# A two-block network kernel on one core: an attention loop and a recurrence are reordered on five engines

## What is computed

```python
def rwkv7_recurrence(r, decay, k, v, a, b):
    """S_t = S_{t-1} diag(decay_t) + (S_{t-1} a_t) b_t^T + v_t k_t^T ;  y_t = S_t r_t."""
...
y = rwkv7_recurrence(rh, dh, kh, vh, -kk, kk * ah)
y = ((y - mu) * lax.rsqrt(var + LNX_EPS)).reshape(B, S, D)
y = y * lnx_w.astype(f32) + lnx_b.astype(f32)
bonus = jnp.sum(rh * kh * r_k.astype(f32), axis=-1, keepdims=True) * vh
y = y + bonus.reshape(B, S, D)
out = (y * g.astype(f32)).astype(w_o.dtype) @ w_o
...
# forgetting attention, 16 heads, two query blocks of 128
s = einsum(q, k) * scale + cum_log_f[q] - cum_log_f[k]
o = softmax(where(causal, s, -inf)) @ v
```

## Time and profile before

| | |
|---|---|
| median of 3 runs | 3367.44 us (3367.32 to 3367.82) |
| the profiled execution, its own time | 3353.73 us |
| its span, first to last instruction | 3352.1 us |
| PE busy | 3220.3 us, 96% |
| DVE busy | 2284.5 us, 68% |
| ACT busy | 1507.4 us, 45% |
| POOL busy | 353.0 us, 11% |
| mean granted TensorE clock | 0.962 of 2.4 GHz |

### The profile page before, as it was taken

One profiled execution on the slowest core, in us unless ns is written; L12 is line 12 of the kernel. 1 busy time (PEld: TensorE's weight loads), 2 busy tenths in 40 slices (PEclk: granted clock), 3 DMA queues, 4 the chain that ended last, 5 costly groups with the idle time before them and its releaser, 6 DMA issues.

```text
span 3352.1 us, 65137 instructions
## 1 busy us (share of the span) xinstructions
PE 3220.3 (96%) x23206; PEld 2785.1 (83%) x23206; DVE 2284.5 (68%) x3387; ACT 1507.4 (45%) x2115; POOL 353.0 (11%) x526
## 2 busy tenths in 40 slices
PE   7999999989998999999999999999999999999998
PEld 6887777878877888888888888888778888888887
DVE  6657666578776776776666767776566766666675
ACT  5543443456645554444443434444344434444343
POOL 2001022000124432100000000200011000000002
PEclk9999999989998888999999999999899999999999
DMA  6654545446761110466666666677435666666664
GB/s 191 171 148 114 138 138 170 132 138 175 210 190 47 34 34 25 139 179 187 185 191 185 191 185 188 176 188 188 119 114 150 181 192 184 191 184 189 186 183 144
DMA packets 1001281, 524.25 MB, mean 156 GB/s; under 512 B 25750, under 2 KB 996396, under 8 KB 1000620
## 3 DMA queue, kind: packets, MB, share of 16 engines
q1 hardware_dynamic: 995756, 507.99, 53.9%
q0 software_dynamic: 4560, 13.05, 1.1%
q10 hardware_dynamic: 816, 1.11, 0.1%
HBM read 513.69 MB, written 8.39 MB: 156 GB/s over the span
## 4 chain that ended last, share of the span: by engine, by line
PE 83%; DVE 8%; issue 4%; ACT 3%; POOL 1%; DMA 0%; ACTq 0%; DVEq 0%; POOLq 0%; SPq 0%; PEldq 0%
PE proj L302 47%; PE proj L304 24%; ACT w_high L271 1%; DVE w_low L258 1%; DVE g L312 1%; DVE w_low L274 1%; PE side L2232 1%; PE side L808 1%; POOL g L1954 0%; PE side L2281 0%; DVE g L2478 0%; DVE g L2702 0%; DVE g L2698 0%; PE side L2362 0%; PE side L2369 0%
## 5 line engine op out<-in xcount | busy, mean ns | idle before, releaser
L302 PE MATMUL proj<-b_pair,w_high 128*128 128x512 f32 x3872 | 1382.7, 401 | 22.8 <-DVE b_pair L1078 8.9
L302 PE MATMUL proj<-a_pair,w_high 128*128 128x512 f32 x3664 | 1293.4, 397 | 39.2 <-DVE a_pair L1692 18.4
L274 DVE TENSOR_TENSOR w_low<-w_raw,w_high 128x1024 fp32r<-128x1024 f32 x688 | 838.0, 1226 | 433.7 <-ACT w_high L271 430.5
L304 PE MATMUL proj<-b_pair,w_low 128*128 128x256 f32 x3872 | 1091.6, 282 | 0.0
L304 PE MATMUL proj<-a_pair,w_low 128*128 128x256 f32 x3664 | 1031.5, 282 | 0.0
L271 ACT ACTIVATE w_high<-w_raw 128x1024 fp32r<-128x1024 f32 x696 | 733.2, 1058 | 563.6 <-PE proj L304 555.6
L302 PEld LDWEIGHTS proj<-b_pair,w_high 128*128 128x128 f32 x3872 | 735.6, 190 | 203.4 <-issue 15.2
L302 PEld LDWEIGHTS proj<-a_pair,w_high 128*128 128x128 f32 x3664 | 692.1, 189 | 201.7 <-issue 22.1
L304 PEld LDWEIGHTS proj<-b_pair,w_low 128*128 128x128 f32 x3872 | 740.6, 191 | 0.2
L304 PEld LDWEIGHTS proj<-a_pair,w_low 128*128 128x128 f32 x3664 | 698.4, 191 | 0.1
L258 DVE TENSOR_TENSOR w_low<-w_raw,w_high 128x1024 fp32r<-128x1024 f32 x276 | 348.7, 1271 | 242.6 <-ACT w_high L252 236.3
(11 more groups left out here) (572 smaller groups left out, 2761.6 us busy)
## 6 DMA issues: line engine op xcount, KB each, us to landing
w_raw<-in_mlp_w_up_dram SPq DMA_DIRECT2D x256, 512.0 KB, 4.2
w_raw<-in_mlp_w_down_dram SPq DMA_DIRECT2D x256, 512.0 KB, 3.9
w_raw<-in_w_in_dram SPq DMA_DIRECT2D x112, 512.0 KB, 3.9
w_raw<-in_rwkv_w_rkv_dram SPq DMA_DIRECT2D x96, 512.0 KB, 4.1
w_raw<-in_w_kvf_dram SPq DMA_DIRECT2D x64, 512.0 KB, 4.1
w_raw<-in_w_out_dram SPq DMA_DIRECT2D x32, 512.0 KB, 3.9
w_raw<-in_rwkv_w_o_dram SPq DMA_DIRECT2D x32, 512.0 KB, 4.4
w_raw<-in_fox_w_q_dram SPq DMA_DIRECT2D x32, 512.0 KB, 3.9
```

The costliest lines, as they stand in the source:

```text
L274: eng.tensor_tensor(wl[slot][:], raw[slot][:], wh[slot][:].bitcast(F32), ALU.subtract)\
L302: pe.matmul(ps[bank][:, :].rearrange("p (a n) -> p a n", a=2), wh[slot][:, k, :], pair[:, :, kk, :], start=kk == 0, stop=False)
L304: mm = pe.matmul(ps[bank][:, 0:S], wl[slot][:, k, :], pair[:, 0, kk, :], start=False, stop=kk == KT - 1)
```

## The change

It reorders; no product, copy or transfer is added or removed.

1. *Gate copied out first.* At level 4 VectorE does `gate_out(fin)` before `whole(i)`, and `low(i - 2)` moves from level 3 to behind level 5.
2. *Reciprocals by halves.* `unit` and `removed` become `removed(j, s)`: half 0 after level 2, half 1 in level 5. `decayed` goes half 0 before it, half 1 behind level 5's copies. VectorE's `bonus` moves ahead of level 5's copies.
3. *Input products inside the last level.* TensorE's L2281 moves from `joint` to level 5, between P and G, where `bonus` stood; `bonus` moves to level 4, behind the G products.
4. *Prologue.* TensorE's `bonus(0)` and `systems(0)` go from chunk 8 to 10, VectorE's from 9 to 11, ScalarE's `lower` from 10 to 12; `rw_begin` moves on TensorE and ScalarE from before turn 0 into its level 1.
5. *Attention.* TensorE's loop is `scores(i, 0)`, half a chunk, `scores(i, 1)`, half a chunk, `values(i)`, half a chunk, `turned(i)`, half a chunk, `output(i)`.

```diff
-            def body(t, n, nh, ring, mh, bank):
+            def body(t, n, nh, ring, mh, bank, middle=None):
...
                     mm.then_inc(sem("w_used"), 1)
+                    if middle and j == 0:
+                        middle()
...
-            fused(pe, project_chunk, scores, (turned, output), forget)
+            def chunk(i, t0, middle):
+                nb, mb = N0["fq"] + t0, M0["fq"] + t0
+                project_chunk(i * 2 + t0, i * 2 + nb, i + nb // 2, nb % 2, i + mb // 2, mb % 2, middle)
+
+            chunk(0, 0, None)
+            chunk(0, 1, None)
+            forget()
+            with pe.Fori(0, 7) as i:
+                scores(i, 0)
+                chunk(i, 2, lambda: scores(i, 1))
+                values(i)
+                chunk(i, 3, lambda: turned(i))
+                output(i)
...
@@ rw_scalar
-                if t == 10:
+                if t == 12:
                     for s in range(2):
                         lower(0, s)
-            rw_begin(act)
...
                     elif lv == 1:
+                        if i == 0:
+                            rw_begin(act)
                         taken(i, "AK")
...
@@ rw_tensor
-            def joint(i):
-                par = i % 2
+            def inputs(i):
                 for s in range(2):
                     b = RW_C[s]
-                    pe.wait_ge(sem("rw_u"), u_done(i, s, 5))
                     pe.wait_ge(sem("rw_masked"), part(i, s, "AK", 6))
                     pe.wait_ge(sem("rw_taken"), part(i, s, "tok"))
                     for h in range(2):
                         mm = pe.matmul(q[3 * s + 2][:, 64 * h:64 * h + 64], b["AK"][:, 2 * h, :], b["tok"][:, 2, rng(h)], start=True, stop=True)
                     mm.then_inc(sem("rw_x"), 1)
+
+            def joint(i):
+                par = i % 2
+                for s in range(2):
+                    pe.wait_ge(sem("rw_u"), u_done(i, s, 5))
                 if i < LAST:
                     systems(i + 1, 0)
...
-                if t == 8:
+                if t == 10:
                     bonus(0)
                     for s in range(2):
                         systems(0, s)
-            rw_begin(pe)
...
                     elif lv == 1:
+                        if i == 0:
+                            rw_begin(pe)
...
-                    elif lv == 5 and i < LAST:
-                        bonus(j)
+                    elif lv == 5:
+                        inputs(i)
...
                     elif lv == 4:
+                        if i < LAST:
+                            bonus(j)
...
@@ rw_vector
-            def unit(j):
...
+            def removed(j, s):
+                t = RW_T[s]
+                dve.wait_ge(sem("rw_max"), pv(j, s))
+                st.need(st.do(dve.reciprocal(t["sq"], t["sq"])))
+                dve.tensor_tensor(t["kk"], t["kk"], t["sq"], ALU.mult).then_inc(sem("rw_kk"), 1)
...
-                if t == 9:
+                if t == 11:
                     bonus(0)
...
                     elif lv == 4:
-                        kw = whole(i)
                         if i:
                             gate_out(fin)
+                        kw = whole(i)
                     elif lv == 5 and i < LAST:
-                        removed(j, ka)
-                        decayed(j)
+                        decayed(j, (0,))
+                        removed(j, 1)
+                        bonus(j)
...
                     elif lv == 2 and i < LAST:
-                        ka = unit(j)
-                    elif lv == 3 and i > 1:
-                        low(i - 2)
+                        removed(j, 0)
                 if i < LAST:
-                    bonus(j)
+                    decayed(j, (1,))
+                if i > 1:
+                    low(i - 2)
```

More of the change, by code:

```diff
@@ L525, in fused_tensor, with scores, values @@
             v = lambda i, s: i * 2 + (s + 1 + HB)
-            def scores(i):
-                for s in range(2):
-                    b = FB[s]
-                    pe.wait_ge(sem("att_staged"), i * 4 + (2 * s + 2 + 2 * HB))
-                    bank = (M0["fq"] + s) % 2
-                    pe.wait_ge(sem(f"proj_out{bank}"), i + ((M0["fq"] + s) // 2 + 1))
-                    for t in range(2):
-                        o = q[s][:, S * t:S * t + FW[t]]
-                        pe.matmul(o, b["qS"][:, P * t:P * t + P], tile(G, i * 2 + s)[:, 0:FW[t]], start=True, stop=False)
-                        mm = pe.matmul(o, selS[s], cneg[:, 0:FW[t]], start=False, stop=True)
-                    mm.then_inc(sem("att_score"), 1)
-            def turned(i):
+            def scores(i, s):
+                b = FB[s]
+                pe.wait_ge(sem("att_staged"), i * 4 + (2 * s + 2 + 2 * HB))
+                bank = (M0["fq"] + s) % 2
+                pe.wait_ge(sem(f"proj_out{bank}"), i + ((M0["fq"] + s) // 2 + 1))
+                for t in range(2):
+                    o = q[s][:, S * t:S * t + FW[t]]
+                    pe.matmul(o, b["qS"][:, P * t:P * t + P], tile(G, i * 2 + s)[:, 0:FW[t]], start=True, stop=False)
+                    mm = pe.matmul(o, selS[s], cneg[:, 0:FW[t]], start=False, stop=True)
+                mm.then_inc(sem("att_score"), 1)
+            def values(i):
                 for s in range(2):
@@ L545, in turned @@
                     mm.then_inc(sem("att_vt"), 1)
+            def turned(i):
                 for s in range(2):
@@ L560, in output @@
                         .then_inc(sem("att_o"), 1)
-            fused(pe, project_chunk, scores, (turned, output), forget)
+            def chunk(i, t0, middle):
[10 more added lines that the diff above has]
+                output(i)
+            scores(7, 0)
+            scores(7, 1)
+            values(7)
+            turned(7)
+            output(7)
         def fused_scalar(act):
@@ L2471, in sums @@
                     dve.tensor_tensor(t["sg"], t["cm"], t["sg"], ALU.subtract).then_inc(sem("rw_cm"), 1)
-            def unit(j):
-                k = []
-                for s in range(2):
-                    t = RW_T[s]
-                    dve.wait_ge(sem("rw_max"), pv(j, s))
-                    k.append(st.do(dve.reciprocal(t["sq"], t["sq"])))
-                return k
+            def removed(j, s):
[3 more added lines that the diff above has]
+                dve.tensor_tensor(t["kk"], t["kk"], t["sq"], ALU.mult).then_inc(sem("rw_kk"), 1)
             def gate_out(i):
@@ L2498, in whole, with decayed @@
                 return k
-            def removed(j, k):
-                for s in range(2):
-                    t = RW_T[s]
-                    st.need(k[s])
-                    dve.tensor_tensor(t["kk"], t["kk"], t["sq"], ALU.mult).then_inc(sem("rw_kk"), 1)
-            def decayed(j):
-                for s in range(2):
+            def decayed(j, only=range(2)):
+                for s in only:
                     t, d = RW_T[s], RW_S[s]
@@ L2604, in rw_vector @@
                 if t == 6:
-                    removed(0, unit(0))
+                    for s in range(2):
+                        removed(0, s)
                 if t == 7:
@@ L2616, in rw_vector @@
                 j, fin, par = i + 1, i - 1, i % 2
-                ka = ks = None
+                ks = None
                 for lv in range(6):
```

## The result

The changed kernel takes 3321.56 us (median of 4 executions, 3318.36 to 3331.26) against 3367.46 for the kernel before (4 executions, 3367.32 to 3367.82): ratio 0.9865, 95% interval 0.985 to 0.9879, 45.9 us less. The forecast was 3339 with a range down to 3325: right in its sign, 17 us short, and the median is outside the range.

The account below looks back on a forecast made before the run. Recurrence bound by TensorE, at half speed in much of each turn's second half, VectorE close behind. Terms 2.1 + 4.9 + 0.3 + 9.0 + 0.5 + 5.5 + 2.7 + 1.5 + 2.5 = 29.0 us gave 3339, range 3325 to 3352.

Parts of the forecast that it names:

- I take the same off both: The sum of 29.0 us comes off the profiled 3353.73 and the median 3367.44 alike, giving 3338.4, say 3339.
- 1.5 and 2.5: Attention's clock gains: rise one step sooner at the start, 1.5 us; 1.5 of three short half-clock stretches gone, 2.5 us.
- Prologue and turn 0: Prologue stall shortened to 2.3 + 3.4 us, 2.1 us off; turn 0, mostly at the hand-over, 4.9 us off.
- 0.3 + 9.0 + 5.5: Turn 1 gives 0.3 us; turns 2 to 6 1.8 each, 9.0; clock falling after level 4, not in it, 5.5.
- case A: Clock stays up in turns 1 to 6, attention's mended too: 39 us, 3328 (3323 with shared interface); chance 19%.
- POOL's `bt`: Input of half 0's `systems` after level 5: ready at 1124.6, asked for at 1126.6, hidden with 2.0 us spare.
- The state copy: Behind level 5: VectorE's queue of 7.5 us reaches it at 1134.1, TensorE's way at 1134.3, a tie; was 1136.16.
- Turn 7: Inputs cost 2.0 us ahead of level 5 and give them back behind it; gate copy's wait gone, 0.5 us gained.
- the 2.7: Attention: 2.8 us of dense products in front of L535's wait for L597, in six of seven places: 2.7 us.
- B: Only waits go and the clock falls as before, attention's too: 19.5 us off, 3348; chance 18%.
- D: VectorE's queue behind level 5 is 2 us longer than 7.5, attention's split costs what its wait did: 3363; chance 6%.
- C: Turns' clock stays low longer, past the joint part: 6 us more a turn leave 8 of 29; chance 7%.

Follow-up runs that it names:

- both_moves: Kernel after, with POOL making the first half's `bt` before waiting for the second half's kk, and VectorE's `low` behind the state copy: 3312.14 us, 0.9858 against the kernel before.
- only_turn: Kernel before with only the turns' edits (gate copy, reciprocals by halves, inputs and `bonus` moved): 3345.92 us, ratio 0.9909.
- only_attention: Kernel before with only the attention edit (scores, `turned` and values split among the half chunks): 3355.76 us, ratio 0.9955.

## Why the prediction was right in sign and short in size

**Two steps failed: the size of the clock's terms, and "I take the same off both".** The forecast fell 17 us short of the measured gain of 45.9, and each of the two is worth about half of that.

The first is in the sum. Against the very profile that I worked from, the four stages gave 37.7 us and not 29.0. The 8.7 missing are those of the half clock: turns 1 to 6 (with a clock's term of 5.5) gave 22.0 instead of 14.8, attention (1.5 and 2.5) 10.9 instead of 6.7, and prologue and turn 7 take 2.7 back.

The second is the way from the profile to the median. The median before lies 13.7 us above its profile, the median after 2.8 below its own, and the unchanged rest of the profile after was 8.3 longer: 13.7 + 2.8 - 8.3 is the other 8.2. I treated the 13.7 as lying in parts that the change leaves alone. Most of it doesn't: the repeated profile of the kernel before has 7.9 us more in the first stage and 3.2 in attention, both at a lower clock, and the change shortens both to below what they are in a fast execution. The first stage is 99.4 to 102.2 in six of the eight profiles with the old hand-over, so typically it gains some 12 us, not 7.

How much belongs to each isn't fixed better than by some us. Repeated profile against repeated profile the four stages give 12.5, 14.8, -3.7 and 14.1 us (the kernel after again: 89.6, 247.9, 37.2 and 140.3), 37.7 in all again, but the stages of one kernel differ by 11.2 us between its two profiles, before and after alike. That the forecast for turns 1 to 6 is hit by this second pair and missed by the first is chance.

Then term by term, against the profile that I worked from:

- *Prologue and turn 0*, 7.0 predicted, 6.1 measured. The stall was shortened to 2.10 and 1.75 us (I had 2.3 and 3.4), and the products at the hand-over start with no wait.
- *Turns 1 to 6*, 14.8 predicted (0.3 + 9.0 + 5.5), 22.0 in one profile of the kernel after and 14.6 in the other (18 on average). The mechanism of level 4 was right: gate copy, `bonus` and inputs stand in turn 2 in the order and without the idle time that I had worked out. The size of the clock's term was off: I took 3.4 us of half clock from each turn, and it is 8 us less a turn in the one profile and 6 in the other. What happened is a mixture of the forecast and case A, turn by turn (in the first profile turn 5 has no half clock, turn 6 13.7 us).
- *POOL's `bt`*, predicted as covered with 2.0 us to spare, holds `systems` for 0.95 us. The absolute times were right: kk of the second half at 1122.8 in the time scale of the profile before is 1118.7 in that of turn 2 after (which begins 4.1 earlier), and POOL starts on it at 1118.86. TensorE got there 3.0 earlier than I had it, as it ran at full clock. A cover that is TensorE's own work shrinks when TensorE gets faster; in case A I should have priced it.
- *The state copy*, predicted as a tie, waits 4.1 us in 3 turns, 7.4 in 4 in the second profile; `low`, which stands ahead of it, takes 1.7 us beside POOL (0.84 and 0.94 for its halves), not the 0.75 that I had for both. The tie was reckoned at half clock, so this too is a point that case A should have priced.
- *Turn 7*, 0.5 predicted, costs 1.3 and, repeated profile against repeated profile, 3.7. Its clock was 0.81 and 0.74 against 0.86 and 0.90. The input products ahead of level 5 are not what costs: in both_moves they stand there too, `low` is behind the state copy, and turn 7 takes 30.7 us at full clock. There TensorE waits 0.4 us for that copy; in both profiles of the kernel after it waits 1.9. So it is `low` ahead of the state copy, as in the point before, with the half clock around it; one profile shows it.

```profile
1284.70:1315.40 30.70, 29.05 (x766) 24.40 (x765) 18.92 (x48) 15.38 (x38) 3.83 (x6) 1.00 0.07 20
```

- *Attention*, 6.7 predicted, 10.9 measured. The wait of L535 went from 3.2 us in seven to 0.4 in one, as the 2.7 had it. The clock's terms, 1.5 and 2.5, are the short ones: the first stretch is 6.83 us instead of 13.6, worth 3.4, and in all 18 us of half clock are gone, worth up to 9.
- *The cases.* B and D fell with only_turn and only_attention. C, a longer low clock, is what turn 7 does, alone. A, at 19%, was the nearest in time (3328, 3323 with the shared interface), though the turns show it in part only.

The Trainium skill ("GPSIMD Engine Reference", Specifications) had GpSimd share SBUF interfaces with VectorE's two-input instructions. The trace after agrees in the main: the pair L2531 takes 0.86 where POOL is idle but for the first 0.14 us, and 1.27 where POOL runs beside nearly all of it, against 1.82 in the earlier trace rows, where it runs beside all of it. The first of the 1.27, though, takes 0.41 of it with POOL's L2005 under way, so not every instruction of the pair is slowed.

Open: what decides in a given turn whether the clock falls, when the order of the instructions is the same in all. The profiles of one kernel differ in it, and no run here sets it.

## What to carry to other kernels

Before a sum from one profile is taken off a median, look at how the profiled execution stands in the scatter, and profile the kernel twice: the stage that differs between the two is where the luck was, and a change there may gain that as well. Where a stretch runs at half clock behind an idle gap, price the whole stretch and not the gap, once as if it stays and once as if it goes; then redo every "covered by TensorE's work" at full clock. Edits that each mend the same half-clock stretch don't add, so try them one by one and leave out those that open a wait of their own.

## What was not expected of the hardware

Products added in idle time made the kernel faster: 3.8 us more of them a turn, 15 us less in all, half clock in turns 1 to 6 from 89 to 0 us in the profiles (mean clock 0.83 and 1.00). And executions of one kernel in one session differ by up to 27 us (3358.7 to 3385.7), while four in another had agreed to 0.5 us. The granted clock shows a part of this. Another part stands at full clock: the same dense products, 391 or 395 ns by their median, which goes with 6.2 us in a stretch of 1025.
